# A conv tap that waits quarter by quarter, and a masked key tile made on GpSimd

## The chip, the cores and the metric

The kernel runs on one core of a Trainium2 chip. A core has a matrix engine (TensorE), a vector engine (VectorE), an activation engine (ScalarE), a general engine (GpSimd) and a queue engine for DMAs (SyncE); in the profile they are PE (PEld for its weight loads), DVE, ACT, POOL and SP. They share the on-chip memory SBUF; TensorE writes to PSUM, whose eight banks VectorE and ScalarE read. The engines run side by side and wait for each other by semaphores. The metric is the device time of one execution in microseconds (us); lower is better.

## The reference

Two layers of a decoder trunk, one inference step, for a prompt of 256 tokens and 8 sample sequences of 8 tokens each (320 columns in all), everything in fp32. Each layer is a half-step feed-forward, a mixer of three head groups, and another half-step feed-forward. The mixer:

```python
def mixer(h, past_k, past_v, s0, buf, past_len, p):
    z = h @ p['w_in']
    gq, gk, gv, gg, glr, sq, sk, sv, cu = jnp.split(z, offs, axis=-1)
    ...
    o_gla, s_new = gla_chunked(q, k, v, log_a, s0)
    ...
    o_sb = stick_breaking(q_sb, k_all, v_all, p['sb_bias'], q_pos, k_pos)
    a, gate = jnp.split(cu, 2, axis=-1)
    u = a * jax.nn.sigmoid(gate)
    y, buf_new = causal_dwconv(u, buf, p['conv_w'], p['conv_b'])
    y = jax.nn.silu(layer_norm(y, p['conv_norm_g'], p['conv_norm_b']))
    mix = jnp.concatenate([o_gla, o_sb, y], axis=-1)
    return mix @ p['w_out'], k_new, v_new, s_new, buf_new
```

Two pieces matter here. The depthwise convolution has 31 taps over 256 channels: y[t] = b + sum over k of w[k] * u[t + k - 30]. And the gated linear attention hands on a state for each sample sequence, S_new = exp(b_last) * S + sum over its 8 tokens of k_t^T v_t.

## The kernel before

**Tiling.** Activations lie transposed, channels on the 128 partitions and the 320 tokens along the free dimension: columns 0 to 255 are the prompt, 256 to 319 the samples. Each weight block of 1024 x 128 is a unit: SyncE loads it into one of eight slots (`raw`), ScalarE makes a rounded copy (`hi`, L1239), VectorE the remainder (`lo`, L1617), and TensorE makes three products for each 128 x 128 tile (`unit`, L605 to L607).

**The mixer's first half** (in layer 0 from about 280 us) runs over the input units m = 7 to 22. TensorE makes unit m and, between its tiles, transposes pages of the key cache and takes their scores. VectorE does for each m a fixed list written out by hand: the `scale` and `decay` of a level of the gated attention, `place_sample` and `place_prompt` (L1842 and L1835, copies of a level's scores from PSUM into `att`, for which TensorE's next level, L845 or L860, waits), `lo` for unit m + 2, `log_weights`, and some taps of the convolution: `TAPS_EARLY` ahead of `place_prompt`, `TAPS_LATE` behind it. TensorE runs its own list in order, so a copy into `att` that comes late stops it.

**A tap** is `conv(k)`: four instructions on VectorE, one for each half of the channels (c) and each of prompt (256 columns) and samples (64 columns) (n). Each takes its part of `yT` (a piece of the tile fT) and adds a shifted piece of `ext` times w[k]. The four write four parts that don't overlap; a part is needed again by the same part of the next tap. `V` is a helper that gives each instruction of VectorE a semaphore count, and `V.settle()` waits for the instruction issued last, whatever it is. It stands once at the head of each tap.

**The mixer's second half** (from about 395 us) has the values of the cache, the prompt's stick-breaking scores and the outputs of the gated attention. On VectorE it begins with the rows n = 0, 1, 2 of the prompt's scores: bias and mask (L1980, or L1984 and L1985), then `ps_t` = min(z, -z) (L1987, signal `pz_neg`); ScalarE takes exp and ln of it, and VectorE adds max(z, 0) (L1994, signal `pz_sp`). TensorE waits for the third `pz_neg` before `gla_means` (L1087), and for the `pz_sp` one by one before the running sums (L1144). Then VectorE makes

```python
V(dve.tensor_tensor(knm[:, :, :], kn[0:TS, 2:3, :].to_broadcast([TS, DB, 256]),
                    cst_("batch_of", TS).unsqueeze(2).to_broadcast([TS, DB, 256]), ALU.mult), sm["knm_ready"])
```

which is L2009: the sample keys `kn` (64 tokens by 256) times a 0/1 mask, eight copies of which each keeps the 8 tokens of one sequence; 64 partitions by 2048 elements. `kn` was copied by ScalarE (signal `knat_ready`). TensorE takes `knm` in `state_products` (L1183), the first of which waits for `knm_ready`. Behind L2009 on VectorE come the last three taps around `gla_read` (L2000), L2018 and the rest.

**GpSimd** clears tiles with memsets at the head of each mixer (L535 to L551) and then issues half of the DMAs of the cache: `keys(h)`, and `values(it)` for it = 0 to 7. values(it) is eight DMAs of 128 KB into one of two buffers, `vpg0b` and `vpg1b` for odd it in layers 0 and 1, each pair of them behind a wait for TensorE to have read values(it - 2) (`v_used`). Its instructions run in order.

Of the kernel before, what the change touches and what calls it, by code (L numbers as in the profile page):

```python
# [14 lines left out]
ALU = mybir.AluOpType  # L15
# [13 lines left out]
DB, DT = 8, 8  # L29
# [188 lines left out]
def build(nc, ins, outs):  # L218
# [123 lines left out]
    def cst_(name, rows=P, cols=None):  # L342
        lo, hi = AT[name]
        return const[0:rows, lo:hi if cols is None else lo + cols]
# [29 lines left out]
    with nc.Block() as block:  # L374
# [103 lines left out]
        def _(pool):  # L478
# [8 lines left out]
            for l in range(L):  # L487
                U = l * U_END

                def at(name, n):  # L490
                    return sm[name], l * per[name] + n
# [77 lines left out]
                        store_rows("v", svn)  # L569
                for it in range(ITS):  # L570
                    values(it)
                pool.wait_ge(*at("s2_ready", 2))
                pool.dma_start(outs["prompt_gla_state"][l, 0].rearrange("(p h) k v -> (h k) p v", p=2), s2[:, :, :]).then_inc(so, 16)
                pool.wait_ge(*at("st_done", 16))
# [1025 lines left out]
        def _(dve):  # L1600
# [178 lines left out]
            for l in range(L):  # L1779
# [4 lines left out]
                def at(name, n):  # L1784
                    return sm[name], l * per[name] + n

                def par(name, c):
                    return par_all[:, l, PAR[name] + c:PAR[name] + c + 1]

                ffn(2 * l, 3 * l, U)  # L1790
                settle_in(M1, U + U_IN)

                def conv(k):

                    V.settle()
                    for c in range(2):
                        v = ext[:, c, HALO + TP:].rearrange("p (b t) -> p b t", b=DB)[:, :, k:k + DT]
                        for n, (out, x) in enumerate(((yT[:, c, 0:TP], ext[:, c, k:k + TP]),
                                       (yT[:, c, TP:T].rearrange("p (b t) -> p b t", b=DB), v))):
                            if k == 0:  # L1800
                                V(dve.tensor_scalar(out, x, par("conv_w", c), par("conv_b", c), ALU.mult, ALU.add))
                            else:
                                V(dve.scalar_tensor_tensor(out, x, par("conv_w", 2 * k + c), out, ALU.mult, ALU.add),  # L1803
                                  sm["conv_y"] if k == TAPS - 1 and c == n == 1 else None)


                def blocks(t, w, half=None):

# [193 lines left out]
                def gla_gated(pair):  # L2002
# [3 lines left out]
                    for h in pair:  # L2006
                        V(dve.tensor_tensor(fT[:, h, :], osq[:, h, :], gate[:, h, :], ALU.mult), sm["o_done"])

                V(dve.tensor_tensor(knm[:, :, :], kn[0:TS, 2:3, :].to_broadcast([TS, DB, 256]),  # L2009
                                    cst_("batch_of", TS).unsqueeze(2).to_broadcast([TS, DB, 256]), ALU.mult), sm["knm_ready"])  # L2010
                if taps < TAPS:
                    conv(taps)
                gla_read((0, 1))
# [92 lines left out]
```

## Time and profile before

| | |
|---|---|
| median of 3 runs | 1406.13 us (1405.67 to 1406.16) |
| the profiled execution | 1406.77 us, of which 1405.1 are the span of the profile |
| TensorE busy | 1381.3 us, 98% of the span |
| VectorE busy | 899.9 us, 64% |
| ScalarE busy | 735.0 us, 52% |
| GpSimd busy | 182.6 us, 13% |
| knm (L2009) | 2.28 us, once in each layer |
| taps (L1803) | 240 instructions, 76.4 us |

How to read it: the span is the time from the first to the last instruction; what lies around it (1.7 us) belongs to the execution but to no instruction. Busy time is the union of an engine's instructions. The records of TensorE overlap, since its products are pipelined; a matrix product of 320 columns shows 0.31 us, and the next starts 0.15 us after it. An idle time in square brackets is that of the engine right before the row, and behind the arrow stands what ended it.

### The profile page before, as it was taken

What the parts mean: (1) busy time and instruction counts of PE and PEld (TensorE: products, weight loads), DVE (VectorE), ACT (ScalarE), POOL (GpSimd) and SP (SyncE); (2) the same over time, 40 slices, a digit from 0 to 9 for tenths busy, and PEclk for the clock granted to TensorE, in tenths of its full rate; (3) what the DMA queues carried; (4) which work ended last, traced back from release to release, by engine and by line L of the source; (5) the groups of instructions that cost most, each with busy time, mean ns of one, the idle gap of its engine ahead of it and who ended that gap; (6) DMA issues with size and microseconds to landing.
All of it is one profiled execution on the core that took longest, in us unless ns stands there. A gap on an engine that the chain in (4) does not pass through costs nothing.

```text
span 1405.1 us, 27974 instructions
## 1 busy us (share of the span) xinstructions
PE 1381.3 (98%) x11063; PEld 1302.6 (93%) x11063; DVE 899.9 (64%) x1508; ACT 735.0 (52%) x1210; POOL 182.6 (13%) x333
## 2 busy tenths in 40 slices
PE   7999999999999999999999999999999999999998
PEld 6999999977878999999999999999788799999998
DVE  5666544669995866663367665346899858756542
ACT  4544343489866554443355444346887665444441
POOL 1020000323262110000000000012333510000000
PEclk9999999999999999999999999999999999999999
DMA  9475455567798595545555554564868895555541
GB/s 245 144 209 150 143 147 157 159 197 229 216 317 262 145 255 150 149 142 150 153 132 151 150 150 139 152 181 139 250 207 252 286 255 155 150 150 148 149 139 50
DMA packets 391558, 249.47 MB, mean 178 GB/s; under 512 B 16513, under 2 KB 379638, under 8 KB 391428
## 3 DMA queue, kind: packets, MB, share of 16 engines
q1 hardware_dynamic: 375602, 204.94, 51.2%
q0 software_dynamic: 15520, 42.62, 9.6%
q8 instruction: 88, 1.44, 0.4%
q14 instruction: 42, 0.34, 0.1%
q10 hardware_dynamic: 306, 0.13, 0.1%
HBM read 242.10 MB, written 5.53 MB: 176 GB/s over the span
## 4 chain that ended last, share of the span: by engine, by line
PE 92%; ACT 2%; DVE 2%; issue 1%; DMA 1%; SPq 0%; POOL 0%; POOLq 0%; DVEq 0%; ACTq 0%
PE bank L605 24%; PE bank L607 24%; PE bank L606 24%; PE bank L763 2%; PE bank L988 2%; PE bank L641 2%; PE bank L645 2%; PE bank L642 2%; PE bank L892 2%; PE bank L1065 1%; ACT kT L1411 1%; DMA raw<-in_ffn_w_gate 1%; PE bank L845 1%; PE bank L969 1%; PE bank L1183 1%
## 5 line engine op out<-in xcount | busy, mean ns | idle before, releaser
L1617 DVE TENSOR_TENSOR w_l<-raw,w_h 128x1024 fp32r<-128x1024 f32 (+1 forms) x332 | 395.6, 1197 | 290.7 <-ACT w_h L1239 290.3
L605 PE MATMUL bank<-hh,w_h 128*128 128x320 f32 x1632 | 513.0, 314 | 0.0
L607 PE MATMUL bank<-hh,w_l 128*128 128x320 f32 x1632 | 504.2, 309 | 0.0
L606 PE MATMUL bank<-hl,w_h 128*128 128x320 f32 x1632 | 504.1, 309 | 0.0
L1239 ACT ACTIVATE w_h<-raw 128x1024 fp32r<-128x1024 f32 (+1 forms) x332 | 332.5, 1030 | 141.2 <-DMA raw<-in_ffn_w_down 100.1
L605 PEld LDWEIGHTS bank<-hh,w_h 128*128 128x128 f32 x1632 | 306.3, 188 | 12.5 <-issue 7.8
L606 PEld LDWEIGHTS bank<-hl,w_h 128*128 128x128 f32 x1632 | 306.5, 188 | 0.6
L607 PEld LDWEIGHTS bank<-hh,w_l 128*128 128x128 f32 x1632 | 306.4, 188 | 0.0
L605 PE MATMUL bank<-guh,w_h 128*128 128x320 f32 x704 | 217.7, 309 | 0.0
L607 PE MATMUL bank<-guh,w_l 128*128 128x320 f32 x704 | 217.3, 309 | 0.0
L606 PE MATMUL bank<-gul,w_h 128*128 128x320 f32 x704 | 217.3, 309 | 0.0
L606 PEld LDWEIGHTS bank<-gul,w_h 128*128 128x128 f32 x704 | 132.2, 188 | 0.0
L605 PEld LDWEIGHTS bank<-guh,w_h 128*128 128x128 f32 x704 | 132.2, 188 | 0.0
L607 PEld LDWEIGHTS bank<-guh,w_l 128*128 128x128 f32 x704 | 132.1, 188 | 0.0
L1324 ACT ACTIVATE sg<-gr 128x320 f32<-128x320 f32 x88 | 41.6, 472 | 170.9 <-DVE gr L1709 170.9
L1329 ACT ACTIVATE guh<-gt 128x320 fp32r<-128x320 f32 x88 | 41.6, 472 | 131.0 <-DVE gt L1720 131.0
L532 POOL DMA_DIRECT2D st<-in_state_gla x4 | 3.6, 897 | 607.1 <-PE bank L607 607.1
L503 POOL DMA_DIRECT2D kpg<-in_cache_sb_k x112 | 60.3, 539 | 154.9 <-PE bank L763 127.9
L1803 DVE SCALAR_TENSOR_TENSOR fT<-ext,par_all,fT 128x256 f32<-128x256 f32 x240 | 76.4, 381 | 2.1
L1709 DVE TENSOR_TENSOR gr<-bank,rs 128x320 f32<-128x320 f32 x88 | 43.0, 488 | 52.7 <-PE bank L607 45.8
L1411 ACT ACTIVATE kT<-bank 128x512 f32<-128x512 f32 x116 | 62.7, 594 | 22.9 <-PE bank L763 22.8
L1718 DVE TENSOR_TENSOR gt<-sg,bank 128x320 f32<-128x320 f32 x88 | 42.7, 485 | 19.8 <-PE bank L607 17.1
(295 smaller groups left out, 1581.4 us busy)
## 6 DMA issues: line engine op xcount, KB each, us to landing
raw<-in_ffn_w_gate SPq DMA_DIRECT2D x88, 512.0 KB, 3.9
raw<-in_ffn_w_up SPq DMA_DIRECT2D x88, 512.0 KB, 3.9
raw<-in_ffn_w_down SPq DMA_DIRECT2D x64, 448.0 KB, 3.7
raw<-in_w_in SPq DMA_DIRECT2D x44, 512.0 KB, 3.9
raw<-in_ffn_w_down SPq DMA_DIRECT2D x32, 512.0 KB, 4.0
kpg<-in_cache_sb_k SPq DMA_DIRECT2D x112, 128.0 KB, 3.3
kpg<-in_cache_sb_k POOLq DMA_DIRECT2D x112, 128.0 KB, 2.6
raw<-in_w_out SPq DMA_DIRECT2D x16, 512.0 KB, 6.9
```

The lines of the kernel that those rows point to most:

```text
L503: pool.dma_start(heads(kpg[l][:, h % 2, b, j, :]), page(pool, ids[4 * i + 2 * (h % 2) + j], ins["cache_sb_k"], l)).then_inc(sm[f"kp_loaded ...
L605: pe.matmul(out, w_h[:, slot, k, :], rhs_h[:, k0 + k, :], start=first, stop=False)
L606: pe.matmul(out, w_h[:, slot, k, :], rhs_l[:, k0 + k, :], start=False, stop=False)
L607: last = pe.matmul(out, w_l[:, slot, k, :], rhs_h[:, k0 + k, :], start=False, stop=end)
L1239: A(nsa(w_h[:, slot, 0:n, :], raw[:, slot, 0:n, :], ACT.Copy), sm["w_hi"])
L1324: A(nsa(sg[:, t, :], gr[:, t, :], ACT.Silu), sm["gate_act"])
L1329: A(nsa(guh[:, 2 * i + t, :], gt[:, t, :], ACT.Copy), sm["gu_hi"])
L1411: A(nsa(half_keys(kT[l][:, h % 2], b), turned_half(2 + b % 2), ACT.Copy), sm["kt_copied"])
L1617: V(dve.tensor_tensor(w_l[:, slot, 0:n, :], raw[:, slot, 0:n, :], w_h[:, slot, 0:n, :].bitcast(F32), ALU.subtract), sm["w_lo"])
L1709: V(dve.tensor_tensor(gr[:, t, :], ffn_bank(i, 2 * t)[:, 0:T], rs[:, :], ALU.mult), sm["gate_r"])
L1718: V(dve.tensor_tensor(gt[:, t, :], sg[:, t, :], ffn_bank(i, 2 * t + 1)[:, 0:T], ALU.mult), sm["gate_up"])
L1803: V(dve.scalar_tensor_tensor(out, x, par("conv_w", 2 * k + c), out, ALU.mult, ALU.add), sm["conv_y"] if k == TAPS - 1 and c == n == 1 else ...
```

## The change

The diff has two parts, and a third that follows from the second.

1. `conv(k)` waits for the last instruction of VectorE only at k = 0. From k = 1 on, each of its four instructions waits for the one that last wrote the same part, whose count is kept in `tapped[c, n]`.
2. The multiply that makes `knm` leaves VectorE.
3. GpSimd makes it, behind the DMAs of values(3) and a wait for `kn`, ahead of those of values(4), with the same operands and the same signal.

```diff
@@ gpsimd
                 for it in range(ITS):
                     values(it)
+                    if it == 3:
+                        pool.wait_ge(*at("knat_ready", 2))
+                        pool.tensor_tensor(knm[:, :, :], kn[0:TS, 2:3, :].to_broadcast([TS, DB, 256]),
+                                           cst_("batch_of", TS).unsqueeze(2).to_broadcast([TS, DB, 256]), ALU.mult).then_inc(sm["knm_ready"], 1)
@@ vector
+                tapped = {}
+
                 def conv(k):
 
-                    V.settle()
+                    if k == 0:
+                        V.settle()
                     for c in range(2):
...
                             if k == 0:
                                 V(dve.tensor_scalar(out, x, par("conv_w", c), par("conv_b", c), ALU.mult, ALU.add))
                             else:
+                                dve.wait_ge(*tapped[c, n])
                                 V(dve.scalar_tensor_tensor(out, x, par("conv_w", 2 * k + c), out, ALU.mult, ALU.add),
                                   sm["conv_y"] if k == TAPS - 1 and c == n == 1 else None)
-
+                            tapped[c, n] = V.last
@@
-                V(dve.tensor_tensor(knm[:, :, :], kn[0:TS, 2:3, :].to_broadcast([TS, DB, 256]),
-                                    cst_("batch_of", TS).unsqueeze(2).to_broadcast([TS, DB, 256]), ALU.mult), sm["knm_ready"])
                 if taps < TAPS:
                     conv(taps)
```

VectorE's queue in layer 0, second half of the mixer, before. L1984 to L1994 are the prompt's scores, L2009 makes knm, L1803 are taps, L2000 is `gla_read`; in brackets is what an instruction waits for:

```order
L1991 SCALAR_TENSOR_TENSOR s_99<-s_98,aend,bank 128x128
L1984 SCALAR_TENSOR_TENSOR ps_z<-bank,sbb_all,const 128x128
L1985 TENSOR_SCALAR ps_z<-bank,sbb_all 128x128
L1984 SCALAR_TENSOR_TENSOR ps_z<-bank,sbb_all,const 128x128
L1985 TENSOR_SCALAR ps_z<-bank,sbb_all 128x128
L1987 SCALAR_TENSOR_TENSOR ps_t<-ps_z 128x512 [waits dve_step]
L1994 SCALAR_TENSOR_TENSOR ps_t<-ps_z,ps_t 128x512 [waits pz_l] x3
L2009 TENSOR_TENSOR knm<-kn,const 64x2048
L1803 SCALAR_TENSOR_TENSOR fT<-ext,par_all,fT 128x256 [waits knm_ready]
L1803 SCALAR_TENSOR_TENSOR fT<-ext,par_all,fT 128x64
L1803 SCALAR_TENSOR_TENSOR fT<-ext,par_all,fT 128x256
L1803 SCALAR_TENSOR_TENSOR fT<-ext,par_all,fT 128x64
```

The same place in the changed kernel (L1995 is the old L1987, L2002 the old L1994, L1811 the old L1803, L2008 the old L2000):

```order
L1995 SCALAR_TENSOR_TENSOR ps_t<-ps_z 128x512 [waits dve_step]
L2002 SCALAR_TENSOR_TENSOR ps_t<-ps_z,ps_t 128x512 [waits pz_l] x3
L1811 SCALAR_TENSOR_TENSOR fT<-ext,par_all,fT 128x256 [waits dve_step]
L1811 SCALAR_TENSOR_TENSOR fT<-ext,par_all,fT 128x64 [waits dve_step]
L1811 SCALAR_TENSOR_TENSOR fT<-ext,par_all,fT 128x256 [waits dve_step]
L1811 SCALAR_TENSOR_TENSOR fT<-ext,par_all,fT 128x64 [waits dve_step]
L2008 SCALAR_TENSOR_TENSOR osq<-bank,par_all,osq 128x320 [waits o_r] x2
```

Between L1994 and the tap nothing is left, the tap's wait for knm's own signal is gone, and all four of its instructions have a wait.

GpSimd's queue at the end of values(3) and the start of values(4), layer 0, before (L359 prepares the address of a page, L355 reads the page numbers):

```order
L517 DMA vpg0b<-in_cache_sb_v 128x256
L359 ISA
L517 DMA vpg0b<-in_cache_sb_v 128x256
L355 TENSOR_LOAD pages x2
L359 ISA [waits v_used]
L517 DMA vpg0a<-in_cache_sb_v 128x256
```

and in the changed kernel:

```order
L517 DMA vpg0b<-in_cache_sb_v 128x256
L359 ISA
L517 DMA vpg0b<-in_cache_sb_v 128x256
L574 ISA
L574 TENSOR_TENSOR knm<-kn,const 64x2048 [waits knat_ready]
L355 TENSOR_LOAD pages x2
L359 ISA [waits v_used]
L517 DMA vpg0a<-in_cache_sb_v 128x256
```

The wait and the multiply have come between the last DMA of values(3) and the first of values(4).

## Rows read from the trace of the kernel before

**Rows 1.** The page, busy time, share of the span and instructions of each engine.

```profile
PE 1381.3 (98%) x11063; PEld 1302.6 (93%) x11063; DVE 899.9 (64%) x1508; ACT 735.0 (52%) x1210; POOL 182.6 (13%) x333
```

**Rows 2.** Stretches: length, busy PE, PEld, DVE, ACT, POOL, then granted clock, DMA share, GB/s.

```profile
280.00:395.00 115.00, 111.61 (x1369) 90.21 (x1369) 99.19 (x206) 97.63 (x190) 38.14 (x71) 1.00 0.74 222
395.00:470.00 75.00, 74.84 (x733) 60.84 (x733) 53.59 (x113) 46.97 (x84) 26.91 (x50) 1.00 0.93 274
...
965.00:1083.00 118.00, 115.18 (x1372) 94.22 (x1371) 101.81 (x212) 95.67 (x186) 39.62 (x73) 1.00 0.77 229
1083.00:1160.00 77.00, 76.92 (x740) 62.06 (x739) 53.93 (x115) 47.69 (x85) 26.50 (x49) 0.98 0.90 267
```

**Rows 3.** Who waited for whom, TensorE, whole run: us in total, times, longest.

```profile
PE bank L860 <- DVE att L1835: 0.7, 2, 0.4
...
PE bank L845 <- DVE att L1842: 0.5, 2, 0.2
```

**Rows 4.** Timeline of TensorE, layer 0: start, us, instruction, count, idle before.

```profile
343.33 0.45 PE L860 MATMUL bank<-qt,kt 64*64 64x64 f32 x8 [0.36 <-DVE att L1835]
```

**Rows 5.** Timeline of VectorE between quarters; then the page's group of all taps.

```profile
344.31 0.28 DVE L1803 SCALAR_TENSOR_TENSOR fT<-ext,par_all,fT 128x64 f32<-128x64 f32 x1
...
344.62 0.48 DVE L1803 SCALAR_TENSOR_TENSOR fT<-ext,par_all,fT 128x256 f32<-128x256 f32 x1
...
345.62 0.28 DVE L1803 SCALAR_TENSOR_TENSOR fT<-ext,par_all,fT 128x64 f32<-128x64 f32 x1
...
345.81 0.29 DVE L1842 COPY_PREDICATED att<-level,bank 64x128 f32<-64x128 uint8 x1
...
L1803 DVE SCALAR_TENSOR_TENSOR fT<-ext,par_all,fT 128x256 f32<-128x256 f32 x240 | 76.4, 381 | 2.1
```

**Rows 6.** Timeline of VectorE ahead of the copy that ends TensorE's wait at 343.33.

```profile
336.39 1.27 DVE L1803 SCALAR_TENSOR_TENSOR fT<-ext,par_all,fT 128x256 f32<-128x256 f32 x4
...
340.75 1.27 DVE L1803 SCALAR_TENSOR_TENSOR fT<-ext,par_all,fT 128x256 f32<-128x256 f32 x4
```

**Rows 7.** Timeline of VectorE, second half of the mixer, layers 0 and 1.

```profile
409.26 0.69 DVE L1987 SCALAR_TENSOR_TENSOR ps_t<-ps_z 128x512 f32<-128x512 f32 x1
...
411.96 2.28 DVE L2009 TENSOR_TENSOR knm<-kn,const 64x2048 f32<-64x2048 f32 x1
...
1096.90 0.69 DVE L1987 SCALAR_TENSOR_TENSOR ps_t<-ps_z 128x512 f32<-128x512 f32 x1
```

**Rows 8.** Timeline of TensorE, second half of the mixer, layers 0 and 1.

```profile
411.01 1.34 PE L1087 MATMUL bank<-osq,const 128*128 128x320 f32 x4
412.19 2.74 PE L1144 MATMUL bank<-ps_t,const 128*128 128x512 f32 x6
...
428.72 1.09 PE L1183 MATMUL bank<-gv,knm 64*64 64x128 f32 x16
...
1098.65 1.34 PE L1087 MATMUL bank<-osq,const 128*128 128x320 f32 x4
```

**Rows 9.** Timeline of GpSimd, its memsets at the head of layer 0's mixer.

```profile
254.81 0.53 POOL L539 MEMSET qb<- 128x512 f32 x1
255.40 1.38 POOL L541 MEMSET att<- 128x1536 f32 x1
```

**Rows 10.** Timeline of GpSimd, DMA issues of values(3), values(5) and layer 1's values(3).

```profile
403.97 4.70 POOL L517 DMA_DIRECT2D vpg0b<-in_cache_sb_v  x8 [0.77 <-issue]
...
417.48 4.70 POOL L517 DMA_DIRECT2D vpg0b<-in_cache_sb_v  x8 [1.66 <-PE bank L988]
...
1094.41 2.35 POOL L517 DMA_DIRECT2D vpg1b<-in_cache_sb_v  x4 [0.36 <-issue]
```

**Rows 11.** DMA issues from 400 to 450: KB each, median us to landing.

```profile
vpg0b<-in_cache_sb_v POOLq DMA_DIRECT2D x24, 128.0 KB, 5.0
```

**Rows 12.** Timeline of VectorE, one instruction during a memset, one after them.

```profile
256.32 0.48 DVE L1652 TENSOR_TENSOR xT<-xT,ht 128x320 f32<-128x320 f32 x1
...
261.63 0.48 DVE L1652 TENSOR_TENSOR xT<-xT,ht 128x320 f32<-128x320 f32 x1
```

## The prediction

> **What bounds the kernel now.** I read the page's table of engines, then the table of stretches, then who waits for whom on TensorE, and only then the timelines of VectorE, GpSimd and TensorE at the places that the diff touches.
>
> TensorE is busy for 1381.3 of the 1405.1 us, VectorE for 899.9 and GpSimd for 182.6 [rows 1]. The table of stretches says what TensorE leaves free: 3.4 us from 280 to 395 and 2.8 from 965 to 1083, where the mixer's input products run, and only 0.16 and 0.08 in the stretches behind them (395 to 470, 1083 to 1160) [rows 2]; most of the rest lies at the program's two ends. So a shorter VectorE gives time back only where TensorE waits for it, and a longer one costs time wherever it makes TensorE wait, since behind such a wait the products are packed.
>
> TensorE waits for VectorE twice in each layer, both times for copies into att: 0.5 us in two waits of L845 and 0.7 in two of L860, 1.2 us in the whole run [rows 3]. In layer 0 the second of them, 0.36 us, ends at 343.33 [rows 4].
>
> **Part 1: a quarter waits for its own quarter only.** A tap is four instructions. The last one (128x64) starts at 344.31 and the next tap, which waits for the instruction right before it, at 344.62: 0.31 us. Where the instruction behind such a quarter waits for something that is long done, it starts 0.19 us later (345.62 to 345.81) [rows 5]. A quarter now waits for one four instructions back, done for over half a microsecond. So each tap begins 0.12 us earlier, and its three added waits are free by that same pair of rows, whose second instruction has a wait too and still overlaps. There are 240 such instructions, 30 taps a layer [rows 5]: 3.6 us of VectorE's time per layer, nearly all of it off the path.
>
> What of it reaches TensorE: between TensorE's two waits in layer 0 VectorE runs without a gap, and two taps (336.39 and 340.75) lie ahead of the copy that ends the second wait [rows 6]. That copy comes 2 x 0.12 = 0.24 us earlier, and TensorE, late by both waits together (0.6), is late by 0.36. Thus 0.24 per layer, **0.5 in all**. The ends are 0 (if the waits cost what they save) and the whole 1.2.
>
> **Part 2a: knm leaves VectorE.** It took 2.28 us, from 411.96, in each layer [rows 7]. TensorE waits for nothing that stands behind it on VectorE, since it idles for 0.16 us in all from 395 to 470 [rows 2]. So on the path this gives 0. knm itself is read at 428.72 [rows 8].
>
> **Part 2b: knm on GpSimd, its length.** No arithmetic of GpSimd is in this trace. Its memsets give the pace of one stream: 512 elements in 0.53 us, 1536 in 1.38, thus 0.83 ns for each and 0.1 us on top [rows 9]; 2048 elements are one stream of 1.8 us. The multiply has two input streams and an output: 3.5 us if the output hides, 5.3 if nothing does. I take the middle, 4.4, since nothing tells the two apart, and keep 1.8 to 5.3 for the range. The Trainium skill has a price: GPSIMD Engine Reference, section Elementwise, side-by-side cycle accounting, gives 4.5 us for an add of two fp32 inputs of 2048 elements; by it the sum below would be 0.2 us larger, and no run here shows it yet.
>
> Its place: behind values(3), whose last DMA issue ends at 408.67 (403.97 plus 4.70) [rows 10]; so from 408.73 to 413.1. The wait for kn that is put ahead of it is met by then: L1991, which VectorE runs before the L1984s that lead to 409.26, already adds up products of kn. Queued behind it on GpSimd are the DMA issues of values(4) and values(5). values(4), again 4.7 us of issues, would end at 418.0; values(5) would start 0.8 later (the 0.77 of idle ahead of 403.97), at 418.8 instead of 417.48, and end at 423.5 [rows 10]. A landing takes 5.0 us from the issue [rows 11], so the last is there at about 428, ahead of TensorE's products with it at about 429.8, right behind the 1.09 us of L1183 [rows 8]. The queue costs 0 then, and begins to cost from a multiply of some 6 us on.
>
> **Part 2c: what VectorE does meanwhile.** At 409.26 it starts the third L1987, then three L1994: each reads two inputs from SBUF. TensorE's L1087 at 411.01 stands behind a wait for that L1987, which ends at 409.95: 1.06 us of room [rows 7, 8]. If VectorE can't read two tiles while GpSimd reads its two, the third L1987 waits until 413.13 and ends at 413.85, and TensorE goes on at 413.9 instead of 411.01: 2.9 us. The chain behind it (ScalarE's exp and ln, L1994, L1144) follows at its old distances, and nothing is given back, because TensorE is packed from there to 470 [rows 2]. In layer 1 GpSimd would begin at 1096.82 (1094.41 plus 2.35 and 0.06) and VectorE's L1987 starts at 1096.90 [rows 7, 10]. If GpSimd comes first, L1987 ends at 1101.95 and TensorE's L1087 moves from 1098.65 to 1102.0: 3.3. If VectorE comes first, GpSimd runs from 1097.6 to 1102.0 and the first L1994 ends at 1102.7; TensorE's L1144, 1.18 us behind L1087 [rows 8] and so at 1099.83, starts at 1102.75: 2.9. I take the second, since the first has 0.08 us in hand.
>
> Do they hold each other up? VectorE's two-input L1652 took 0.48 us at 256.32, in the middle of GpSimd's 1.38 us memset, and 0.48 us again at 261.63 [rows 9, 12]: writes of GpSimd disturb nobody. Of its reads no row speaks. A rule of the Trainium skill does: SBUF, State Buffer, section Who interferes with whom, says that a VectorE instruction with two inputs in SBUF contends with a GpSimd instruction that reads SBUF, not with one that only writes, and that the later one stands until the other is through. By it the time is the one worked out here, without it that of rival 1. The memset rows agree with its second half; no run here shows the first.
>
> **The sum.** 2.9 + 2.9 - 0.5 = +5.3 us. The profiled span is 1405.1 and that execution's own time 1406.77, 0.6 above the median of the runs, 1406.13; the difference is added to the median: **1411.4**. By the ends of the multiply's length: 1.8 us leaves 0.3 per layer (1406.2), VectorE's own 2.3 leaves 0.8 (1407.2), 5.3 makes 3.8 (1413.2).
>
> **Rival 1, no hold.** Both engines read side by side, and only part 1 is left: 1405.6, not slower, with ends 1404.9 and 1406.1. For it: the memset rows, and GpSimd's DMA issues, which fill 38 and 27 us of the two mixer stretches of layer 0 [rows 2] beside a VectorE that is never seen waiting for GpSimd. Against it: those are all writes or issues. It decides by whether L1987 keeps its 0.69 us.
>
> **Rival 2, a partial hold.** The two only slow each other, or VectorE's queue wins and GpSimd gets in late, between the L1994s. VectorE then loses 1 to 2.5 us near TensorE's waits, TensorE 0.3 to 2.4 per layer, say 1.4: 1408.4.
>
> **Rival 3, the added waits are not free.** If each of the four emptied the pipeline, a tap would lose 4 x 0.12 instead of 0.12: 10.8 us of VectorE per layer. Two taps add 0.7 us to TensorE's wait at 343.33, and the ten or so that follow while VectorE has no gap add 3.6: some 1414 without a hold. Against it: 345.62 and 345.81 [rows 5].
>
> **Rival 4, a slow multiply.** At 7.5 us GpSimd issues values(5) so late that TensorE stands some 1.5 us at 429.8, in each layer: 1408.6 without a hold. Against it: even three passes make 5.3.
>
> **How the numbers follow.** Forecast 50%, rival 1 36%, rival 2 9%, rival 3 2%, rival 4 3%. I put the hold above its absence because GpSimd's two input streams and VectorE's two-input instructions fall on the same 4 us and no row shows two such readers side by side, but the trace leaves it open. What a measurement of this kernel can tell from no change is about 0.2%, 2.8 us: 1403.3 to 1408.9. The forecast's own range is 1409.5 to 1413.2. Slower: the forecast but for a short multiply (48), half of rival 2 and of rival 4 (6) and rival 3 (2), 56%; same: rival 1 and the rest, 42%; faster 2%. Since rival 1 holds over a third, the range reaches to it: 1405.0 to 1412.8, which leaves out the upper end of the multiply's length and the lower part of rival 1.
>
> **What would show it.** The multiply's start near 408.7 and its duration on GpSimd; the third L1987 starting or ending near 413.8, and close to 2.9 us of idle TensorE ahead of L1087; 0.19 us instead of 0.31 between taps; TensorE's 0.36 at 343.33 cut to about 0.2 (it comes 0.12 earlier itself); the landings of values(5) ahead of TensorE. I am wrong if L1987 keeps its length and place while GpSimd multiplies, or if the taps don't close up.

## The result

Measured side by side on one chip, ten runs each, the kernel before takes 1405.9 us in the median (1403.36 to 1409.47) and the changed kernel 1410.29 (1407.75 to 1411.12). The ratio of the two is 1.0024, with a 95% interval of 1.0014 to 1.0034: the change costs 2 to 5 us. The forecast was 1411.4, its range 1405.0 to 1412.8.

The page of the changed kernel (its own time 1410.56, against 1406.77 of the execution that was profiled before), busy time of each engine:

```profile
span 1408.7 us, 27976 instructions
...
PE 1382.5 (98%) x11063; PEld 1302.9 (92%) x11063; DVE 896.5 (64%) x1506; ACT 734.1 (52%) x1210; POOL 189.8 (13%) x335
```

Against [rows 1] VectorE is busy for 3.4 us less, GpSimd for 7.2 more (two multiplies), and the span is 3.6 longer. Line numbers of the changed kernel are 4 higher than before ahead of the taps and 8 higher from the taps on: L1803 is now L1811, L1987 is L1995, L1994 is L2002. On TensorE L860 is L864, L988 is L992, L1087 is L1091 and L1144 is L1148.

Who waited for whom on TensorE (us in total, times, longest), the changed kernel:

```profile
PE bank L1091 <- DVE ps_t L1995: 2.7, 2, 1.9
...
PE bank L864 <- DVE att L1843: 0.5, 2, 0.3
```

The first line is new. The second is the old wait of L860 in [rows 3], 0.7 before; the wait of L845 is gone from the list. So this one list shows both halves of the change: what the quarters gave, and what the move took.

The place of the loss, layer 0. GpSimd, then VectorE, then TensorE (start, duration, instruction, count, idle before it):

```profile
404.08 4.70 POOL L517 DMA_DIRECT2D vpg0b<-in_cache_sb_v  x8 [0.77 <-issue]
408.92 3.59 POOL L574 TENSOR_TENSOR knm<-kn,const 64x2048 f32<-64x2048 f32 x1
412.48 4.33 POOL L517 DMA_DIRECT2D vpg0a<-in_cache_sb_v  x8
```

```profile
408.99 0.34 DVE L1993 TENSOR_SCALAR ps_z<-bank,sbb_all 128x128 f32<-128x128 f32 x1
409.37 3.70 DVE L1995 SCALAR_TENSOR_TENSOR ps_t<-ps_z 128x512 f32<-128x512 f32 x1
412.99 1.28 DVE L2002 SCALAR_TENSOR_TENSOR ps_t<-ps_z,ps_t 128x512 f32<-128x512 f32 x2
```

```profile
409.25 1.93 PE L992 MATMUL bank<-vpg0a,wT 128*32 128x256 f32 x32
413.12 1.67 PE L1091 MATMUL bank<-osq,const 128*128 128x320 f32 x4 [1.94 <-DVE ps_t L1995]
414.58 4.15 PE L1148 MATMUL bank<-ps_t,const 128*128 128x512 f32 x6
```

GpSimd multiplies from 408.92 to 412.51. VectorE's bias add from PSUM runs inside that time and keeps its 0.34 us. The instruction behind it has two inputs in SBUF (z and z) and is on the engine for 3.70 us instead of the 0.69 of [rows 7]; it ends at 413.07, 0.56 behind the multiply. TensorE, ready at 411.18, starts the output means 1.94 us late. In layer 1 VectorE's instruction starts 0.08 us behind the multiply and stands for nearly all of it:

```profile
1099.92 3.59 POOL L574 TENSOR_TENSOR knm<-kn,const 64x2048 f32<-64x2048 f32 x1
...
1100.00 4.07 DVE L1995 SCALAR_TENSOR_TENSOR ps_t<-ps_z 128x512 f32<-128x512 f32 x1
```

**A ledger of TensorE.** I paired the products of the two profiles one by one, and list by how much the changed kernel's start lies behind (the line numbers are those of the kernel before):

| place (start before, after) | behind by | what came in since the row above |
|---|---|---|
| L860, 343.33, 343.55 | 0.22 | 0.46 from the first wait for w_l at the program's start (1.0 us instead of 0.4), less 0.24 from the quarters at L845 and L860 |
| L860, 351.59, 351.70 | 0.11 | the quarters once more: -0.11 |
| L1087, 411.01, 413.12 | 2.11 | the stall: 2.00 |
| L1148, 414.77, 418.57 | 3.81 | the six products of L1144 take 4.15 us instead of 2.74, at the lower clock: 1.70 with the last of L1087 |
| first product of unit work, 445.04, 448.52 | 3.48 | the kernel before waits there for values (0.16 of idle time shown), the changed kernel does not: -0.33 |
| L860 of layer 1, 1030.98, 1034.19 | 3.21 | the quarters at L845 and L860: -0.25 |
| L860, 1039.24, 1042.34 | 3.11 | the quarters once more: -0.11 |
| L1087, 1098.65, 1104.12 | 5.47 | the stall of layer 1, with what the lower clock hides of it: 2.36 |
| L1171, 1113.91, 1117.78 | 3.86 | the kernel before had its own stretch at the lower clock here: -1.61 |
| end of the span | 3.58 | -0.28 |

The quarters show at a third place in each layer, 351.59 and 1039.24, which the list of PE's waits doesn't name: TensorE stood there for 0.04 us before,

```profile
350.48 1.07 PE L892 MATMUL bank<-kT,qb 128*32 128x256 f32 x16
351.59 0.45 PE L860 MATMUL bank<-qt,kt 64*64 64x64 f32 x8
```

and now starts 0.07 ahead of the end of L892's record, as products do that wait for nothing. The quarters give 0.35 us in layer 0 and 0.36 in layer 1, 0.71 in all.

Two kinds of entries stand in the ledger: stalls and quarters, which belong to the change, and stretches at the lower clock, which come and go. Their granted clock, in stretches of the changed kernel and then of the kernel before (length, busy PE, PEld, DVE, ACT, POOL, granted clock, DMA share, GB/s):

```profile
411.00:414.00 3.00, 1.06 (x7) 0.68 (x4) 3.00 (x3) 0.87 (x2) 3.00 (x4) 1.00 1.11 324
414.00:417.40 3.40, 3.40 (x6) 1.60 (x5) 3.25 (x9) 3.29 (x6) 2.81 (x6) 0.50 1.09 348
...
1100.00:1103.50 3.50, 3.40 (x32) 1.36 (x31) 3.50 (x1) 0.88 (x3) 3.50 (x2) 0.51 1.08 342
```

```profile
1108.00:1112.00 4.00, 4.00 (x38) 3.16 (x38) 3.49 (x9) 3.27 (x6) 1.69 (x4) 0.74 1.07 350
1112.00:1116.00 4.00, 4.00 (x25) 2.49 (x26) 2.18 (x4) 3.58 (x7) 0.00 (x0) 0.83 0.36 123
```

A share of 0.50 is the lower level, 1.2 instead of 2.4 GHz. In layer 1 of the changed kernel it falls on the products ahead of the stall:

```profile
1099.89 3.51 PE L992 MATMUL bank<-vpg1a,wT 128*32 128x256 f32 x32
1104.12 1.34 PE L1091 MATMUL bank<-osq,const 128*128 128x320 f32 x4 [0.72 <-DVE ps_t L1995]
```

The 32 products of L992 take 3.51 us instead of the 1.93 of layer 0, so TensorE arrives 1.58 late by itself and shows only 0.72 of idle time; without that stretch it would have waited 2.3. The sum of the waits, 2.7, therefore shows too little, and what the change costs in this profile is, by the ledger, 2.00 + 2.36 - 0.71 = 3.65 us. The ratio says 3.4 (2.0 to 4.8).

### The profile page after: what moved, and what is told of

Same layout as the page of the kernel before. It is cut to its first block, busy times and chain, and to the rows that moved or that the text cites. A ratio compares the mean times of both kernels' runs of the same rounds, so it can differ in the third digit from the quotient of the medians.

```text
span 1408.7 us, 27976 instructions
## 1 busy us (share of the span) xinstructions
PE 1382.5 (98%) x11063; PEld 1302.9 (92%) x11063; DVE 896.5 (64%) x1506; ACT 734.1 (52%) x1210; POOL 189.8 (13%) x335
## 4 chain that ended last, share of the span: by engine, by line
PE 92%; DVE 4%; ACT 2%; issue 1%; DMA 1%; SPq 0%; DVEq 0%; ACTq 0%
PE bank L609 24%; PE bank L611 24%; PE bank L610 24%; PE bank L767 2%; PE bank L992 2%; PE bank L645 2%; PE bank L649 2%; PE bank L646 2%; PE bank L896 2%; ACT kT L1415 1%; DVE ps_t L1995 1%; PE bank L1109 1%; DMA raw<-in_ffn_w_gate 1%; PE bank L1111 1%; PE bank L1110 1%
## 5 line engine op out<-in xcount | busy, mean ns | idle before, releaser
L1811 DVE SCALAR_TENSOR_TENSOR fT<-ext,par_all,fT 128x256 f32<-128x256 f32 x240 | 74.2, 377 | 0.0
```

## The experiments

Theory A is the forecast's: while GpSimd runs an instruction that reads SBUF, VectorE's instruction that needs two SBUF reads stands until it is over. The rivals blame the taps' waits, GpSimd's queue with its transfers, the mere load on GpSimd's write side, TensorE's clock, or the length of the multiply. A ratio is always to runs of the kernel before on the same chip.

**The quarters alone.** knm stays on VectorE.

```diff
-                    V.settle()
+                    if k == 0:
+                        V.settle()
...
+                                dve.wait_ge(*tapped[c, n])
...
+                            tapped[c, n] = V.last
```

> Part 1 alone: the taps wait quarter by quarter, knm stays on VectorE. Theory A (GpSimd's multiply holds up VectorE's two-input instructions, and TensorE's wait for the third L1987 is the loss): 0.5 us faster than before (1405.4 where before gives 1405.9), taps 0.20 us behind each other's last quarter instead of 0.31, TensorE's wait near 343.3 down from 0.36 to 0.25 us, the 0.24 us one near 338.2 gone, no idle of TensorE ahead of gla_means near 411. Theory B (the added waits of the taps cost the time): 2 to 4 us slower than before.

Measured: 1406.07 us, ratio 0.9997 (0.9987 to 1.0007). The waits of TensorE in it, and VectorE's third min(z,-z):

```profile
PE bank L988 <- DMA vpg1b<-in_cache_sb_v: 1.2, 1, 1.2
...
PE bank L860 <- DVE att L1839: 0.5, 2, 0.3
```

```profile
409.40 0.69 DVE L1991 SCALAR_TENSOR_TENSOR ps_t<-ps_z 128x512 f32<-128x512 f32 x1
```

The wait for att is that of the changed kernel, L1991 keeps its 0.69 us, and nothing is listed ahead of L1087. Paired with the kernel before, TensorE gains 0.24 us up to 343.33 and 0.24 up to 1030.98, as worked out, and 0.11 more at 351.59 and at 1039.24: 0.70 in all. The ratio can't tell that from nothing. The head of a tap follows the quarter before it by 0.196 us instead of 0.316, in all 20 places where tap follows tap, and the other 40 heads too start some 0.08 us ahead of the end of the record before them, where they started 0.04 behind it. The new first line is a warning: in layer 1 TensorE came 2.2 us earlier than in the profile of before (most of it because that one had its stretch at the lower clock there), met values that had not landed, and stood 1.2 us for them. Here 1.1 of the 2.2 us won ahead of a transfer were lost at it.

**The move alone.** The taps as before; knm on GpSimd behind values(3).

```diff
                     values(it)
+                    if it == 3:
+                        pool.wait_ge(*at("knat_ready", 2))
+                        pool.tensor_tensor(knm[:, :, :], kn[0:TS, 2:3, :].to_broadcast([TS, DB, 256]), ...
...
-                V(dve.tensor_tensor(knm[:, :, :], kn[0:TS, 2:3, :].to_broadcast([TS, DB, 256]),
-                                    cst_("batch_of", TS).unsqueeze(2).to_broadcast([TS, DB, 256]), ALU.mult), sm["knm_ready"])
```

> Part 2 alone: knm on GpSimd behind values(3), each tap waits once at its head as in before. Theory A: the same 3.0 us hold of the third row's min(z, -z) on VectorE (3.7 us long instead of 0.69), TensorE idle 1.9 us ahead of gla_means in layer 0, and 0.5 us slower than the changed kernel: 4 us above before. Theory B: as before, within 1 us.

Measured: 1411.21 us, ratio 1.0029 (1.0019 to 1.0040): the whole loss is there without the quarters, and the old waits for att are back (0.8 and 0.5 us). GpSimd, VectorE, TensorE:

```profile
408.58 3.59 POOL L574 TENSOR_TENSOR knm<-kn,const 64x2048 f32<-64x2048 f32 x1
```

```profile
409.04 3.69 DVE L1993 SCALAR_TENSOR_TENSOR ps_t<-ps_z 128x512 f32<-128x512 f32 x1
```

```profile
408.93 3.38 PE L992 MATMUL bank<-vpg0a,wT 128*32 128x256 f32 x32
412.79 1.34 PE L1091 MATMUL bank<-osq,const 128*128 128x320 f32 x4 [0.48 <-DVE ps_t L1993]
```

The lower clock stands on L992 (3.38 us), ahead of the idle time, not behind it. By the pairing TensorE loses 2.00 us at L1087 of layer 0 and 2.36 at that of layer 1, the stretch at the lower clock included: what it loses in the changed kernel.

**Writes instead of a multiply.** GpSimd fills knm with zeros twice, 3.6 us in all, quarters kept. The masked keys are left out, so the products for the sample states are made of zeros; every instruction behind stays.

```diff
-                        pool.tensor_tensor(knm[:, :, :], kn[0:TS, 2:3, :] ..., ALU.mult)
+                        pool.memset(knm[:, :, :], 0.0).then_inc(sm["knm_ready"], 1)
+                        pool.wait_ge(*at("knm_ready", 1))
+                        pool.memset(knm[:, :, :], 0.0).then_inc(sm["knm_ready"], 1)
```

> The changed kernel, but GpSimd's multiply is left out and two memsets of knm stand in its place (so the sample states lack this layer's keys): 2 x 1.8 = 3.6 us of GpSimd at the same place, the DMAs behind it as late, but nothing read from SBUF. Theory A (a reader holds a two-input reader): the third min(z, -z) keeps 0.69 us, TensorE has no idle ahead of gla_means, time 0.5 us below before. Theory C (any work of GpSimd there costs, by its DMA issues that come late or by its writes): as the changed kernel, 3 to 4 us above before.

Measured: 1405.22 us, ratio 0.9996 (0.9984 to 1.0007). GpSimd and VectorE:

```profile
408.02 1.80 POOL L574 MEMSET knm<- 64x2048 f32 x1
409.88 1.80 POOL L576 MEMSET knm<- 64x2048 f32 x1
```

```profile
408.57 0.69 DVE L1996 SCALAR_TENSOR_TENSOR ps_t<-ps_z 128x512 f32<-128x512 f32 x1
```

GpSimd is busy as long as with the multiply, its transfers are queued behind just as long, and the loss is gone. What holds VectorE is that GpSimd reads; that its transfers come late costs nothing here.

**One input instead of two.** GpSimd copies kn into all eight parts of knm; the mask is left out.

```diff
-                        pool.tensor_tensor(knm[:, :, :], kn[0:TS, 2:3, :] ..., ALU.mult)
+                        pool.tensor_copy(knm[:, :, :], kn[0:TS, 2:3, :].to_broadcast([TS, DB, 256]))
```

> The changed kernel, but GpSimd copies kn into the eight parts of knm instead of multiplying by the mask (the mask is left out): one input stream instead of two, some 1.9 us by the memset's pace. Theory A in its plain form (every instruction of GpSimd that reads SBUF holds): the third min(z, -z) begins at 409.4 and ends near 408.9 + 1.9 + 0.6 = 411.4, 2.0 us long, TensorE idle about 0.2 us ahead of gla_means, time near before. Theory A2 (only a two-input instruction of GpSimd holds): 0.69 us, no idle. Theory D (VectorE is only slowed while both read, in proportion): the min(z, -z) 1.2 to 1.4 us.

Measured: 1406.9 us, ratio 1.0001 (0.9990 to 1.0011).

```profile
407.80 1.89 POOL L574 COPY knm<-kn 64x2048 f32<-64x2048 f32 x1
```

```profile
408.34 1.90 DVE L1994 SCALAR_TENSOR_TENSOR ps_t<-ps_z 128x512 f32<-128x512 f32 x1
```

```profile
408.23 3.43 PE L991 MATMUL bank<-vpg0a,wT 128*32 128x256 f32 x32
411.59 1.49 PE L1090 MATMUL bank<-osq,const 128*128 128x320 f32 x4
```

One read stream is enough: L1994 takes 1.90 us instead of 0.69 and ends at 410.24, 0.55 behind the copy, 1.21 us late. TensorE has 1.06 us of room there (part 2c), and in this profile it comes later still, since L991 ran at the lower clock; no idle time is listed, and the ratio shows no loss. In layer 1 the same instruction takes 2.33 us, and there too products at the lower clock come ahead of TensorE's arrival: without them it would have waited, by an estimate from these records, 0.1 us in layer 0 and 0.5 in layer 1. The hold is there and cheap; that this profile shows it free is in part the clock's doing.

**The multiply at a place where nothing hurries.** Quarters kept; the multiply moves behind values(5), and waits for VectorE's first copy of sample outputs.

```diff
-                    if it == 3:
+                    if it == 5:
                         pool.wait_ge(*at("knat_ready", 2))
+                        pool.wait_ge(*at("so_done", 1))
```

> Quarters kept; GpSimd makes the masked keys after values(5)'s transfers instead of values(3)'s, and waits besides for VectorE's first copy of sample outputs, so that the multiply runs at about 423.7 to 427.3, between the last key-side work and the state products at 428.9. Theory A (a GpSimd instruction that reads SBUF holds VectorE's instructions with two SBUF inputs until it ends): the multiply takes 3.6 us again and now holds the second subtraction that makes w_l (425.30 in the kernel with the quarters alone, 1.23 us), which ends about 0.55 us after the multiply, at 427.8, 1.3 us late; TensorE needs what follows it only 2 to 4 us later, so that no idle time of TensorE behind VectorE is left, neither of 1.94 us before the scan of ps_t nor elsewhere. Time as with the quarters alone, 1405.5 to 1406.6, ratio 0.9990 to 1.0005. Rival P (the loss goes with the multiply's engine, wherever it stands, as queue time or as lower clock): 1409 to 1411, ratio 1.002 to 1.003.

Measured: 1406.69 us, ratio 1.0001 (0.9991 to 1.0010).

```profile
423.49 3.59 POOL L575 TENSOR_TENSOR knm<-kn,const 64x2048 f32<-64x2048 f32 x1 [0.25 <-DVE fT L1977]
```

```profile
423.15 0.85 DVE L1977 COPY fT<-bank 64x32 f32<-64x32 f32 x4 [0.37 <-PE bank L1098]
426.22 1.95 DVE L1622 TENSOR_TENSOR w_l<-raw,w_h 128x1024 fp32r<-128x1024 f32 x1 [2.22 <-ACT w_h L1244]
```

The same 3.59 us, and it still holds an instruction: w_l takes 1.95 us instead of 1.23 and ends at 428.17, 1.09 behind the multiply. The copies from PSUM run inside it undisturbed. No wait of TensorE came of it, and the loss is gone, so it went with the place and not with the engine. Nor is there a gain: VectorE's 2.28 us were worth nothing, as part 2a said.

**Half of the multiply.** GpSimd masks four sequences at the changed kernel's place, VectorE the other four at the old one.

```diff
-                        pool.tensor_tensor(knm[:, :, :], kn[0:TS, 2:3, :].to_broadcast([TS, DB, 256]), ...
+                        pool.tensor_tensor(knm[:, 4:8, :], kn[0:TS, 2:3, :].to_broadcast([TS, 4, 256]), ...
...
+                V(dve.tensor_tensor(knm[:, 0:4, :], kn[0:TS, 2:3, :].to_broadcast([TS, 4, 256]), ...
```

> Quarters kept; GpSimd masks the keys of four of the eight sequences only, at the place of the changed kernel, and VectorE masks the other four at the old place. Theory A: the half takes 1.8 to 1.9 us (half of 3.59), ends at about 410.8, and VectorE's third min(z,-z) ends 0.55 us later, at 411.3 (length about 1.95 us instead of 3.70); TensorE came to it at 411.15 with nothing in the way, so that it waits 0.1 to 0.3 us instead of 1.94. Time 1406 to 1407.3, ratio 1.0000 to 1.0010: less than a quarter of the stall for half of the multiply, since the first 1.1 us of lateness are free. Rival L (the loss grows with the length of the multiply): half of the changed kernel's loss, 1408.3, ratio 1.0014. Rival F (a fixed price of any GpSimd multiply there): ratio 1.0024.

Measured: 1407.25 us, ratio 1.0006 (0.9996 to 1.0015).

```profile
409.44 1.89 POOL L574 TENSOR_TENSOR knm<-kn,const 64x1024 f32<-64x1024 f32 x1
```

```profile
409.89 1.99 DVE L1995 SCALAR_TENSOR_TENSOR ps_t<-ps_z 128x512 f32<-128x512 f32 x1
```

```profile
411.93 1.34 PE L1091 MATMUL bank<-osq,const 128*128 128x320 f32 x4 [0.22 <-DVE ps_t L1995]
```

Layer 0 is theory A's to a tenth: 1.89, 1.99, 0.22. In layer 1 L1995 takes 2.38 us, and TensorE came late by itself (L992 at the lower clock, 3.33 us), so that no wait is shown; with 1.93 us for L992 it would have waited an estimated 0.6. The fixed price (1.0024) is outside the interval; that of half the loss (1.0014) lies just inside it, so here the idle time decides, 0.22 against 1.94, and not the ratio.

**The lateness without GpSimd.** Quarters kept, GpSimd makes nothing; VectorE itself masks keys ahead of the third min(z,-z), four sequences of them twice.

```diff
+                    if n == 2:
+                        dve.wait_ge(*at("knat_ready", 2))
+                        for b0, b1 in ((4, 8), (0, 8)):
+                            V(dve.tensor_tensor(knm[:, b0:b1, :], ..., ALU.mult), sm["knm_ready"])
+                            V.settle()
                     V(dve.scalar_tensor_tensor(ps_t[:, n, :], ps_z[:, n, :], -1.0, ps_z[:, n, :], ALU.mult, ALU.min), sm["pz_neg"])
```

> Quarters kept; GpSimd makes nothing: VectorE itself makes the masked keys ahead of its third min(z,-z), four sequences of them twice (some 1.2 + 2.3 us), so that min(z,-z) comes as late as in the changed kernel. Theory A: min(z,-z) keeps 0.69 us but ends at 413.0 to 413.6, TensorE waits 1.9 to 2.4 us for it, and the time is that of the changed kernel, 1409 to 1411, ratio 1.0022 to 1.0036: the lateness of this one result is the loss. Rival Q (the loss comes from GpSimd's queue, the transfers behind its multiply): nothing is queued there, 1406, ratio 0.9995 to 1.0005, although TensorE waits.

Measured: 1410.44 us, ratio 1.0026 (1.0017 to 1.0036).

```profile
407.96 3.52 DVE L1993 TENSOR_TENSOR knm<-kn,const 64x1024 f32<-64x1024 f32 x2
411.60 0.69 DVE L1997 SCALAR_TENSOR_TENSOR ps_t<-ps_z 128x512 f32<-128x512 f32 x1
```

```profile
412.34 1.34 PE L1087 MATMUL bank<-osq,const 128*128 128x320 f32 x4 [2.45 <-DVE ps_t L1997]
```

The instruction keeps its 0.69 us and is merely late; TensorE waits 2.45 and 2.44 us, and the time is that of the changed kernel. Whatever makes this one result late by that much costs this much: the lateness is enough for the loss, without GpSimd's queue, behind which nothing stands here. That the queue adds nothing in the changed kernel either is what the memsets showed.

**Is it the two inputs?** The changed kernel, with the third min(z,-z) written as min(-z,0), one SBUF input. This part of the computation is changed where z is negative; size and place stay.

```diff
-                    V(dve.scalar_tensor_tensor(ps_t[:, n, :], ps_z[:, n, :], -1.0, ps_z[:, n, :], ALU.mult, ALU.min), sm["pz_neg"])
+                    if n == 2:
+                        V(dve.tensor_scalar(ps_t[:, n, :], ps_z[:, n, :], -1.0, 0.0, ALU.mult, ALU.min), sm["pz_neg"])
```

> The changed kernel, but VectorE's third min(z,-z), an instruction with two SBUF inputs (z and z), is written as min(-z,0), with one SBUF input; this leaves a part of the computation changed (the last four rows' heads of min(z,-z) where z is below 0), the size and the place of the instruction stay. Theory A in its narrow form (held are VectorE's instructions with two SBUF inputs, no others): the instruction runs in 0.3 to 0.7 us inside GpSimd's multiply, TensorE's wait of 1.94 us at the output means is gone, and the next instruction with two SBUF inputs, the first max(z,0)+ln, is held instead until 0.55 us after the multiply, some 413.1, while TensorE comes to its product at 412.33: 0.7 to 0.8 us of idle time there in each layer. Time 1407 to 1408.3, ratio 1.0005 to 1.0014. Theory A wide (every VectorE instruction that reads SBUF alone is held): wait and time of the changed kernel, ratio 1.0022 to 1.0030.

Measured: 1409.41 us, ratio 1.0018 (1.0009 to 1.0027).

```profile
408.69 3.59 POOL L574 TENSOR_TENSOR knm<-kn,const 64x2048 f32<-64x2048 f32 x1
```

```profile
409.15 3.42 DVE L1996 TENSOR_SCALAR ps_t<-ps_z 128x512 f32<-128x512 f32 x1
412.50 1.28 DVE L2005 SCALAR_TENSOR_TENSOR ps_t<-ps_z,ps_t 128x512 f32<-128x512 f32 x2
```

```profile
412.63 1.34 PE L1091 MATMUL bank<-osq,const 128*128 128x320 f32 x4 [1.66 <-DVE ps_t L1996]
...
1101.67 1.34 PE L1091 MATMUL bank<-osq,const 128*128 128x320 f32 x4 [2.03 <-DVE ps_t L1996]
```

The ratio lies between the ranges of the two forms and its interval reaches into both; the trace decides. The narrow form of theory A fell: an instruction with a single SBUF input is held as well. It ends 0.29 us behind the multiply, where the two-input form ends 0.55 behind and w_l, of 1.23 us, 1.09. The last two are the instruction's own length less 0.14; if that holds for this one too, its own length is 0.43, some two thirds of the 0.69, an estimate, since no run has it undisturbed. It would then run at a faster pace than the two-input form, and may need both of VectorE's ways to read SBUF for that. The trace of the kernel before has such a pace: a copy of 128x240 from SBUF to SBUF takes 0.285 us (L1891), one of 128x256 out of PSUM 0.423 (L1958); but a tensor_scalar of 128x256 from SBUF to SBUF with its two factors in SBUF takes 0.409 (L1801), so not every one-input instruction has it. The Trainium skill says so (SBUF — State Buffer, section on SBUF's two separate sides: the lock also concerns a VectorE instruction in a mode that uses two ports); the hold agrees, though no run here reads the mode itself. What ran inside a multiply undisturbed, in all profiles, reads PSUM: L1993 here, the copies at 423.15 above.

**Is the wait for min(z,-z) all of it?** The changed kernel, with TensorE's wait ahead of the output means moved from the third min(z,-z) to VectorE's last read of z out of PSUM.

```diff
-                pe.wait_ge(*at("pz_neg", 3))
+                pe.wait_ge(*at("pz_read", 1))
...
-                            V(dve.tensor_scalar(o[:, P:TP], i[:, P:TP], bias, None, ALU.add))
+                            if h == 3:
+                                V(dve.tensor_scalar(o[:, P:TP], i[:, P:TP], bias, None, ALU.add), sm["pz_read"])
```

> The changed kernel with one wait of TensorE moved: ahead of the output means it waits for VectorE's last read of z out of the banks (a semaphore of its own on the last bias add) instead of for the third min(z,-z) behind it; everything is computed. Theory A: VectorE's min(z,-z) is held as before (3.6 to 3.7 us, to about 413.07), but TensorE runs the means at 411.2 and waits only at the product of ps_t, which comes at 412.33 and needs the first max(z,0)+ln, held behind min(z,-z) to some 413.7 (the two of them 1.28 us from 412.99): 1.2 to 1.4 us idle in each layer instead of 1.94. Time 1408 to 1409.5, ratio 1.0012 to 1.0021. Rival M (the wait for min(z,-z) is the whole of the loss, what stands behind it has slack): ratio 0.9995 to 1.0003.

Measured: 1408.96 us, ratio 1.0016 (1.0007 to 1.0025).

```profile
411.33 1.34 PE L1091 MATMUL bank<-osq,const 128*128 128x320 f32 x4
413.94 1.55 PE L1148 MATMUL bank<-ps_t,const 128*128 128x512 f32 x3 [1.26 <-DVE ps_t L2005]
```

The means run on time, and the next reader of VectorE's chain waits instead, 1.26 us in layer 0 and 1.62 in layer 1. By the pairing TensorE loses 1.53 and 1.89 us there, where the changed kernel loses 2.00 and 2.36 (the records of L1087 and L1144 overlap by more than those ahead of L1087, so idle time tells less at L1144). Moving the wait saves 0.47 us in each layer, about a quarter of the stall; the rest is the chain's, so rival M fell.

Neither this profile nor that of the one-input kernel has a stretch at the lower clock between 280 and 1400 us, and both kernels are slower than the one before with the interval above 1: the loss doesn't need the clock.

All of it side by side. "Idle" is TensorE's idle time at L1087 or L1144 behind VectorE, both layers:

| kernel | idle, us | ratio |
|---|---|---|
| quarters alone | 0 | 0.9997 |
| memsets | 0 | 0.9996 |
| copy | 0 | 1.0001 |
| multiply behind values(5) | 0 | 1.0001 |
| half a multiply | 0.22, none shown | 1.0006 |
| wait moved | 1.26, 1.62 | 1.0016 |
| one-input min | 1.66, 2.03 | 1.0018 |
| changed kernel | 1.94, 2.30 (0.72 of it shown) | 1.0024 |
| late on VectorE | 2.45, 2.44 | 1.0026 |

From no idle to 4.9 us of it the ratio rises by 0.0029, 4.1 us, in the order of the idle times, though the intervals of neighbours overlap. The move alone (1.0029) shows 0.48 and 0.76 with the lower clock ahead of it in both layers, so its row can't be placed by the idle time; by the pairing it stands beside the changed kernel, with 2.00 and 2.36 each.

## Why the prediction was right

- **Bound, and the worth of VectorE's time: right.** Taking 2.28 us off VectorE gave nothing: the kernel with the multiply behind values(5) has them off VectorE and stays at 1.0001.
- **The quarters: right where worked out, and a third place was missed.** 0.24 us in each layer up to 343.33 and 1030.98, for 0.24 worked out. Another 0.11 came in each layer at 351.59 and 1039.24: the forecast read the list of PE's waits, in which an idle time of 0.04 us doesn't stand, and took two waits a layer for all of them. The term is 0.7 instead of 0.5. The rest of TensorE's wait at 343.33 is still there, 0.26 after 0.36. The page's group of all taps reads

```profile
L1811 DVE SCALAR_TENSOR_TENSOR fT<-ext,par_all,fT 128x256 f32<-128x256 f32 x240 | 74.2, 377 | 0.0
```

with 74.2 us instead of 76.4 and none of the 2.1 us of idle time ahead of it [rows 5]: 4.3 us of VectorE, where 3.6 a layer, 7.2, had been worked out. The row shows only part of it: it doesn't count where a tap's head now overlaps an instruction of another group, as 40 of the 60 heads can. Head by head the 0.12 us are there at all 60: 7.1 us. So the term was right. The added waits are free: rival 3 fell with the quarters alone.
- **The hold: right, and the step with the least evidence.** The forecast took it on a rule of the Trainium skill (SBUF — State Buffer, section Who interferes with whom) and gave it 50%. The traces agree with both halves of the rule: a GpSimd instruction that reads holds, one that only writes doesn't. Memsets of the same length that leave L1996 at 0.69 us, against 3.70 under the multiply, show that. Rival 1 (no hold) and rival 2 (a share of the speed each) fell: the instruction doesn't run slower, it ends at a fixed 0.55 us behind GpSimd's.
- **The length of the multiply: too long.** 3.59 us for 4.4. The middle between 3.5 (two input streams, the output hidden) and 5.3 had no evidence, and the measured length lies at the first. The Trainium skill gives 4.5 us for an add of two fp32 inputs of 2048 elements (GPSIMD Engine Reference, section Elementwise, side-by-side cycle accounting); this multiply, on 64 partitions and with broadcast inputs, measures less, and the measurement decides. With 3.59 the sum's own working would have given 2.9 - 0.8 = 2.1 in layer 0; the pairing shows 2.00, with 1.94 of idle time.
- **Layer 1: the other order.** I let VectorE come first there (2.9 us). GpSimd began at 1099.92, 0.08 ahead of L1995 at 1100.00, and the instruction stood for all of it. With the true length the branch that the forecast set aside gives 3.3 - 0.8 = 2.5; the pairing shows 2.36. The forecast's choice was a guess, made against the 0.08 us that its own rows gave GpSimd. In all seven profiles with GpSimd's work behind values(3) GpSimd came first in layer 1, but by no more than 0.05 to 0.11 us.
- **The queue behind the multiply: right at 0.** No wait for values stands in the changed kernel's list in either layer. The multiply didn't even set when values(5) was issued: GpSimd was through with values(4) early enough to wait 4.47 us for TensorE before it, and issued it at 421.28 (forecast 418.8), as late as TensorE itself. Rival 4 had no case.
- **Nothing given back: right as far as shown.** 0.33 us came back ahead of 445.04, where the kernel before had waited for values. But the quarters alone, only 0.14 us behind the kernel before there, don't wait either and gain 0.37, so this belongs to the one profile of before and not to the stall.
- **The sum: right in sign, too large.** 2.0 + 2.4 - 0.7 = 3.7 us in place of 5.3. The length of the multiply takes 1.6 off; the other errors nearly cancel: 0.4 more for the order in layer 1, 0.2 less for the quarters, 0.2 less in the two stalls. The runs give 3.4 by the ratio and 4.4 by the medians (1405.9 and 1410.29). The forecast's distance of 1.1 us to the measured time flatters it: the sum was off by 1.6.

What stays open is the lower clock. Stretches of it, 3.4 us each, sit in the mixer's second half in six of the eleven profiles: after the stall in layer 0 of the changed kernel, ahead of it in layer 1 and in both layers of the move alone, at 409 in the copy and in the multiply behind values(5), where nothing stalls, at 1097 in the half multiply, and in the kernel before at 1109.9 too. The kernel with the longest stalls (2.45 and 2.44) has none, nor have the one-input kernel and the one with the wait moved, which have GpSimd's full multiply behind values(3). So neither a stall nor the multiply is enough to bring them; whether the multiply makes them likelier can't be said, since one profile of each kernel is too few.

## What to carry to other kernels

Before work is moved to GpSimd to relieve VectorE, list what VectorE runs beside it. While GpSimd read SBUF, each VectorE instruction that took both inputs from SBUF stood until GpSimd was through (min(z,-z) behind values(3), w_l behind values(5)), and so did the one with a single input that was tried. The price is what is left of GpSimd's instruction when VectorE's comes, less the room that the reader of its result has. Put such work where VectorE reads PSUM or where its results are needed late; the same 3.59 us cost 2.0 to 2.4 us a layer behind values(3) and no measurable time behind values(5). No run here has VectorE's instruction begin first. And VectorE's 2.28 us were worth nothing, since TensorE waited for nothing behind them: look for a wait for VectorE in the list before you take time off it.

## What the hardware showed that I had not expected

A one-input GpSimd copy (1.89 us) holds VectorE like the multiply does, and a one-input VectorE tensor_scalar of 512 fp32 elements from SBUF to SBUF is held like a two-input one. The end of the held instruction lies at a fixed distance behind GpSimd's end, in both layers of each kernel: 0.55 us for an instruction of 0.69, 1.09 for one of 1.23, which is its own length less 0.14.

The scatter of this kernel goes largely with TensorE's clock. Of 29 runs of the kernel before on one chip, the 4 with a mean granted clock of 1.0 average 1404.6 us, the 4 with 0.996 average 1409.0. One such stretch at 1.2 GHz costs about 1.6 us where TensorE is packed (1.70 and 1.61 in the ledger), and less ahead of a stall, which swallows it. A look at layer 0 of one pair of profiles would have put 1.7 us of clock down to the change.
